# Gate rows of a three-layer kernel: by way of DRAM in place of VectorE and PE

## The reference

```python
def adaln(cond, w, b):
    return jnp.split(jax.nn.silu(cond) @ w + b, 6, axis=-1)

def modulate(x, shift, scale):
    return rms_norm(x) * (1.0 + scale) + shift
```

## Time and profile before

| | before |
|---|---|
| median of three runs | 3646.86 us |
| profiled execution | 3648.11 us |
| span of its instructions | 3646.3 us |
| PE busy | 3121.2 us (86%) |
| VectorE busy | 1479.6 us (41%) |
| ScalarE busy | 889.9 us (24%) |
| GpSimd busy | 290.6 us (8%) |
| DMA queue of SP | 190288 packets, 647.72 MB |
| granted TensorE clock, mean | 0.92 |
| `gate_rows` on VectorE, L552 (64 instructions) | 12.9 us |

### The profile page before, as it was taken

One profiled execution on the slowest core, in us unless ns is written; L12 is line 12 of the kernel. 1 busy time (PEld: TensorE's weight loads), 2 busy tenths in 40 slices (PEclk: granted clock), 3 DMA queues, 4 the chain that ended last, 5 costly groups with the idle time before them and its releaser, 6 DMA issues. The chain is left out here.

```text
span 3646.3 us, 95140 instructions
## 1 busy us (share of the span) xinstructions
PE 3121.2 (86%) x42406; PEld 2257.6 (62%) x42406; DVE 1479.6 (41%) x2409; ACT 889.9 (24%) x1501; POOL 290.6 (8%) x241
## 2 busy tenths in 40 slices
PE   6978879997877888787897956676999999999996
PEld 3855558886565666674786945533566666666663
DVE  3355653333663554546565885524111111111111
ACT  2114322222222343331343532301000011100000
POOL 0020200000311132230000013100000000000000
PEclk7989789999898999997998967887999999999998
DMA  7252332222133100103653520221999999999993
GB/s 285 82 172 81 133 139 93 93 93 93 45 142 124 50 21 29 42 4 124 231 185 119 196 82 3 100 98 38 399 408 407 405 405 406 406 406 408 406 405 148
DMA packets 220725, 684.12 MB, mean 188 GB/s; under 512 B 26096, under 2 KB 51184, under 8 KB 187712
## 3 DMA queue, kind: packets, MB, share of 16 engines
q1 hardware_dynamic: 190288, 647.72, 46.4%
q10 hardware_dynamic: 30192, 32.77, 2.6%
HBM read 659.46 MB, written 20.97 MB: 187 GB/s over the span
## 5 line engine op out<-in xcount | busy, mean ns | idle before, releaser
L3466 PE MATMUL experts_psum_gu<-ring,experts_x 128*32 128x256 f32 x9216 | 507.6, 381 | 13.8 <-ACT experts_x L3510 13.8
L3466 PEld LDWEIGHTS experts_psum_gu<-ring,experts_x 128*32 128x32 f32 x9216 | 296.8, 111 | 216.2 <-ACT experts_x L3510 15.4
L3570 DVE TENSOR_TENSOR experts_gate<-experts_psum_gu,experts_bias 128x768 f32<-128x768 f32 x32 | 30.6, 957 | 863.9 <-PE experts_psum_gu L3466 863.9
L3489 PE MATMUL experts_psum_down<-experts_weights,experts_hiddenT 128*32 128x256 f32 x6144 | 339.1, 381 | 4.2 <-ACT experts_hiddenT L3518 4.2
L3489 PEld LDWEIGHTS experts_psum_down<-experts_weights,experts_hiddenT 128*32 128x32 f32 x6144 | 200.6, 111 | 136.8 <-issue 6.0
L818 PE MATMUL mlp_psum_bank<-mlp_x_high,mlp_w_high 128*128 128x512 f32 (+1 forms) x512 | 175.6, 343 | 12.6 <-DVE xT_rounded L322 12.6
L296 DVE TENSOR_TENSOR ring_rounded<-ring,mlp_w_high 128x1024 fp32r<-128x1024 f32 x128 | 156.7, 1226 | 50.6 <-ACT mlp_w_high L291 50.5
L3514 ACT ACTIVATE experts_sigmoid<-experts_gate 128x768 f32<-128x768 f32 x32 | 27.0, 843 | 615.3 <-DVE experts_gate L3572 615.3
L818 PE MATMUL mlp_psum_bank<-xT_rounded,mlp_w_high 128*128 128x512 f32 (+1 forms) x512 | 173.8, 339 | 0.0
L818 PE MATMUL mlp_psum_bank<-mlp_x_high,ring_rounded 128*128 128x512 f32 (+1 forms) x512 | 173.2, 338 | 0.0
L3466 PE MATMUL experts_psum_gu<-xT,experts_x 128*32 128x256 f32 x3072 | 171.6, 379 | 0.0
(11 more groups left out here) (724 smaller groups left out, 5796.5 us busy)
## 6 DMA issues: line engine op xcount, KB each, us to landing
ring<-in_w_gu SPq DMA_DIRECT2D x186, 1024.0 KB, 18.0
experts_weights<-in_w_down SPq DMA_DIRECT2D x128, 1024.0 KB, 19.4
ring<-in_ada_w SPq DMA_DIRECT2D x36, 2048.0 KB, 8.7
ring<-in_mlp_w SPq DMA_DIRECT2D x32, 2048.0 KB, 8.0
xT<-in_w_gu SPq DMA_DIRECT2D x64, 1024.0 KB, 18.9
ring<-in_w_in SPq DMA_DIRECT2D x12, 2048.0 KB, 7.6
ring<-in_ab_w_in SPq DMA_DIRECT2D x6, 2048.0 KB, 9.7
ring<-in_w_rkv SPq DMA_DIRECT2D x6, 2048.0 KB, 8.5
```

Source lines behind the costliest of these rows:

```text
L3466: mm = nc.tensor.matmul(pg[o, q, gr, :], x, w[:, c:c + C], start=(u == 0 and gr != 1), stop=(u == U - 1), skip_group_check=True)
L3489: mm = nc.tensor.matmul(pd[o, gr, :], hidT[:, ch, gr, GROUP * v:GROUP * v + GROUP], w[:, ch, C * c:C * c + C], start=(v == 0 and ch == 0 a ...
L3570: v.tensor_tensor(gt[:, :, :], pg[:, 0, 0:GROUPS, :], rep(bias[:, 0, :], GROUPS), ALU.add).then_inc(s_bg, 1)
```

## The change

The four `gate_rows` phases are gone. In their place each gate takes two DMA steps on SP's queue. First its columns are stored to a row of DRAM (`gate_out`): the source is 128 x 8 single values, one every 8 bytes in a partition, the target has the values of one partition 512 bytes apart, so that the store is made of 1024 pieces of 4 bytes. Later, in another phase, the row of 4 KB is read to all 128 partitions (`gate_in`, 512 KB for a gate). Where `rows1` stood, a `load` phase is left that does the same loads as before.

| gate | stored in | loaded in |
|---|---|---|
| layer 0, four | `mlrows`, after `sel` and `head_row`, ahead of the bias and the ring loads | `about`, ahead of the ring loads |
| layer 1, two | `norm1a` | `rwout`, ahead of the ring loads |
| block 2, mixer | `norm2a`, last of the Fetch | `gdmerge`, with `sn` |
| block 2, experts | `mixout`, ahead of the ring loads | `norm2m`, last of the Fetch |

`gemm_tok` gets a Fetch: SP issues it first, and VectorE waits for it ahead of the first output tile. In `gemm_rows` and in `norm1a` SP waits for the store at the end of its program.

```diff
@@ class Fetch
-        for dst, src in self.jobs:
-            eng.dma_start(dst, src).then_inc(self.sem, 16)
+        for dst, src, *by_element in self.jobs:
+            eng.dma_start(dst, src, allow_slow_non_contiguous=bool(by_element)).then_inc(self.sem, 16)
@@ gemm_tok(..., fetch=None)
             def _(sync):
+                if fetch is not None:
+                    fetch.issue(sync)
                 ring.issue(sync, len(chunks))
...
                         dve.wait_ge(ring.gemm_done, done0 + n + 1)
+                        if n == 0 and fetch is not None:
+                            fetch.wait(dve)
                         out(ch, t, c0, w, banks[:, n % 8, 0:w]).then_inc(evac, 1)
@@
-def gate_rows(g, name, cols, rows, fetch=None):
...
+def gate_out(g, dram, layer, gates):
+    return [(dram[n].rearrange("(k p) -> p k", p=P).unsqueeze(2), g.mods[layer % 2][:, 8 * j:8 * j + 8, i:i + 1], True) for n, j, i in gates]
+
+def gate_in(dram, rows, gates):
+    return [(rows[:, k, :], row(dram[n])) for k, n in enumerate(gates)]
@@ gemm_rows(..., fetch)
             def _(sync):
+                fetch.issue(sync)
                 ring.issue(sync, n_chunks)
+                fetch.wait(sync)
@@ layer0
-                       Fetch(g, "ldsel", [(sel[:, :, :], a["sel"]), (head_row[:, :], row(a["headn"]))]),
+                       Fetch(g, "ldsel", [(sel[:, :, :], a["sel"]), (head_row[:, :], row(a["headn"]))]
+                             + gate_out(g, gate_d, 0, ((0, 2, 0), (1, 2, 1), (2, 5, 0), (3, 5, 1)))),
...
-        gate_rows(g, "rows0", [lambda kt, j=j, i=i: g.mods[0][:, 8 * j + kt, i:i + 1] for j, i in
-                               ((2, 0), (2, 1), (5, 0), (5, 1))], rows)
         gemm_tok(g, "about", widths(D), (g.xT, g.xT_low), ALL_TILES,
-                 residual(g, lambda t: rows[:, 0 if t >= 2 else 1, :], 0))
+                 residual(g, lambda t: rows[:, 0 if t >= 2 else 1, :], 0), fetch=Fetch(g, "ldgate0", gate_in(gate_d, rows, range(4))))
@@ layer1
+    norm_T(g, "norm1a", ALL_TILES, g.xT, lambda t: mod(1, t), lambda t: mod(0, t),
+           fetch=Fetch(g, "stgate1", gate_out(g, gate_d, 1, ((0, 2, 0), (1, 5, 0)))))
...
-            gate_rows(g, "rows1", [lambda kt, j=j: g.mods[1][:, 8 * j + kt, 0:1] for j in (2, 5)], rows,
-                      Fetch(g, "ldro", [(g2a[:, :], a["g2"][0:P, :]), (g2b[:, :], a["g2"][P:G_LORA, :])]
+            load(g, "ldro", [(g2a[:, :], a["g2"][0:P, :]), (g2b[:, :], a["g2"][P:G_LORA, :])]
...
-                     residual(g, lambda t: rows[:, 0, :], 0))
+                     residual(g, lambda t: rows[:, 0, :], 0), fetch=Fetch(g, "ldgate1", gate_in(gate_d, rows, range(2))))
@@ block2
                                              (small[:, :], row(a["small2"])), (gn[:, :], row(a["gdn_norm_g"]))]
+                               + gate_out(g, gate_d, 2, ((0, 2, 0),))))
...
+                gd_merge(..., Fetch(g, "ldmix", [(sn[:, :], row(a["ssd_norm_g"]))] + gate_in(gate_d, rows, (0,))),
...
-                gate_rows(g, "rows2", [lambda kt: g.mods[0][:, 16 + kt, 0:1]], rows)
-                gemm_rows(g, "mixout", 4, mixT, rows[:, 0, :])
+                gemm_rows(g, "mixout", 4, mixT, rows[:, 0, :], Fetch(g, "stgate3", gate_out(g, gate_d, 2, ((1, 5, 0),))))
...
+                   fetch=Fetch(g, "ldmoe", [(rb[:, :], row(a["router_b"])), (iota[:, :], row(a["iota"]))] + gate_in(gate_d, rows, (1,))))
-            gate_rows(g, "rows3", [lambda kt: g.mods[0][:, 40 + kt, 0:1]], rows)
```

More of the change, by code:

```diff
@@ L326, in get, with gemm_tok @@
         return self.hi[:, kt, sl], self.x_low[:, kt, sl]
-def gemm_tok(g, name, chunks, acts, tiles, out, depth=8):
+def gemm_tok(g, name, chunks, acts, tiles, out, depth=8, fetch=None):
     nc, ring = g.nc, g.ring
@@ L3117, in _, with gemm_rows @@
                 m.add(dve)
-def gemm_rows(g, name, n_chunks, actT, row):
+def gemm_rows(g, name, n_chunks, actT, row, fetch):
     nc, ring = g.nc, g.ring
@@ L3694, in layer0 @@
     nc = g.nc
+    gate_d = nc.dram_tensor("gates_0", [4, D], F32, kind="Internal").ap()
     first_modulation(g, "ada0", (a["cond_col"], a["cond2_col"]), a["adab_col"][0], ident, const, x_in)
@@ L3756, in layer1 @@
     mod = lambda j, t: g.mods[1][:, 8 * j:8 * j + 8, 0 if t >= 2 else 1]
-    norm_T(g, "norm1a", ALL_TILES, g.xT, lambda t: mod(1, t), lambda t: mod(0, t))
     scr = {n: nc.dram_tensor(f"rw_{n}", [2 if n == "r" else 4, P, D], F32, kind="Internal").ap()
            for n in ("k", "v", "kk", "r")}
+    gate_d = nc.dram_tensor("gates_1", [2, D], F32, kind="Internal").ap()
+    norm_T(g, "norm1a", ALL_TILES, g.xT, lambda t: mod(1, t), lambda t: mod(0, t),
+           fetch=Fetch(g, "stgate1", gate_out(g, gate_d, 1, ((0, 2, 0), (1, 5, 0)))))
     with ExitStack() as outer:
@@ L3801, in layer1 @@
             roT_low = rounded_alias(nc, roT)
-            gate_rows(g, "rows1", [lambda kt, j=j: g.mods[1][:, 8 * j + kt, 0:1] for j in (2, 5)], rows,
-                      Fetch(g, "ldro", [(g2a[:, :], a["g2"][0:P, :]), (g2b[:, :], a["g2"][P:G_LORA, :])]
-                            + [(v[:, t, :], scr["v"][2 + t]) for t in range(2)]
-                            + [(lw[:, :], row(a["lnx_w"])), (lb[:, :], row(a["lnx_b"]))]))
+            load(g, "ldro", [(g2a[:, :], a["g2"][0:P, :]), (g2b[:, :], a["g2"][P:G_LORA, :])]
+                 + [(v[:, t, :], scr["v"][2 + t]) for t in range(2)]
+                 + [(lw[:, :], row(a["lnx_w"])), (lb[:, :], row(a["lnx_b"]))])
             rw_readout(g, y, coef, v, {"lw": lw[:, :], "lb": lb[:, :]}, sg0, sg1, g2a, g2b, ro,
@@ L3817, in block2 @@
     nc = g.nc
+    gate_d = nc.dram_tensor("gates_2", [2, D], F32, kind="Internal").ap()
     mod = lambda j, t: g.mods[0][:, 8 * j:8 * j + 8, 0]
@@ L3829, in block2 @@
                    fetch=Fetch(g, "ldconv", [(gains[:, :, :], a["norm_g_col"]), (taps[:, :, :], a["taps_col"]), (cbias[:, :], a["cbias_col"]),
-                                             (small[:, :], row(a["small2"])), (gn[:, :], row(a["gdn_norm_g"]))]))
+                                             (small[:, :], row(a["small2"])), (gn[:, :], row(a["gdn_norm_g"]))]
+                               + gate_out(g, gate_d, 2, ((0, 2, 0),))))
             p2 = msb("proj2", [P, 2, 2080])
@@ L3862, in block2 @@
                 sn = isb("sn", [P, D])
-                gd_merge(g, p2, og, ys, {"gn": gn[:, :], "sn": sn[:, :]}, mix, Fetch(g, "ldmix", [(sn[:, :], row(a["ssd_norm_g"]))]),
+                rows = isb("gate_rows2", [P, 1, D])
+                gd_merge(g, p2, og, ys, {"gn": gn[:, :], "sn": sn[:, :]}, mix, Fetch(g, "ldmix", [(sn[:, :], row(a["ssd_norm_g"]))] + gate_in(gate_d, rows, (0,))),
                          (2, 8, 4, a["adab2_col"]))
@@ L3867, in block2 @@
                                   for t in range(2) for k in range(16)])
-                rows = isb("gate_rows2", [P, 1, D])
-                gate_rows(g, "rows2", [lambda kt: g.mods[0][:, 16 + kt, 0:1]], rows)
-                gemm_rows(g, "mixout", 4, mixT, rows[:, 0, :])
+                gemm_rows(g, "mixout", 4, mixT, rows[:, 0, :], Fetch(g, "stgate3", gate_out(g, gate_d, 2, ((1, 5, 0),))))
         acc = osb("moe_acc", [P, 2, D])
@@ L3881, in block2 @@
             norm_T(g, "norm2m", LAT_TILES, g.xT, lambda t: mod(4, t), lambda t: mod(3, t), gains[:, 1, :], off=2,
-                   fetch=Fetch(g, "ldmoe", [(rb[:, :], row(a["router_b"])), (iota[:, :], row(a["iota"]))]))
-            gate_rows(g, "rows3", [lambda kt: g.mods[0][:, 40 + kt, 0:1]], rows)
+                   fetch=Fetch(g, "ldmoe", [(rb[:, :], row(a["router_b"])), (iota[:, :], row(a["iota"]))] + gate_in(gate_d, rows, (1,))))
             router(g, a["router_w"], rb[:, :], iota[:, :], a["b_down"], acc, rank[:, :, :], topg[:, :, :], XgT,
```

## The result

The changed kernel is slower, by little. Its median is 3650.07 us (20 runs, 3643.34 to 3658.74) against 3642.46 us for the kernel before (20 runs, 3635.29 to 3650.76): ratio 1.002, 95% interval 1.0012 to 1.0028, thus 7.3 us slower, from 4.4 to 10.2. The profiled execution took 3649.26 us.

The account below looks back on a forecast made before the run. Phases end in barriers, so wall time between barriers, not PE's 86% busy time, was taken to price the change. 21.4 - 1.6 - 5.2 - 2.0 = 12.6 us less, from 3646.9 to 3634.3 us; range 3627 to 3652.

Parts of the forecast that it names:

- The phases that go: Wall time saved by removing the four `gate_rows` phases: 12.0 + 0 + 3.7 + 5.7 = 21.4 us.
- clock charge: At the start of `mixout`, PE would run some 3.3 us at half clock after the pause, costing 1.7 us.
- The loads of the rows: Rows loaded in `about`, `rwout` and `gdmerge` would be hidden, 0 each; the one in `norm2m` would cost 1.6 us.
- S: Time one store of 1024 4-byte pieces takes on the queues: taken as 2.0 us, bounds 1.0 to 5.5.
- -(4S - 2.8): In `mlrows`, four stores ahead of the ring load delay the fourth slice: -5.2 us, bounds -1.2 and -19.2.
- low bound: Time per store from below, by comparing the loads `router_w` and `gains`: 1024 pieces take about 1.0 us more than none.
- The room of 2.8 us: In `mlrows`, free queue time between `head_row` leaving the engines at about 349.0 and the ring load beginning at 351.8.
- The signs named beforehand: Prediction wrong if a lone store takes 6 us or more, SP is held issuing one, or VectorE waits in `about`.
- "Slower": Rival: writes of neighbouring values wait for each other, felt in `mlrows`' queue; S = 7 gives 3659.3 us; chance 0.10.
- "Even": Rival: S is 3.1 to 6.0, both DMA waits give back the savings; S = 4.5 gives 3646.9 us; chance 0.18.

Follow-up runs that it names:

- e2: The kernel before with only the four layer 0 stores added to `mlrows`, read by nothing; 3665.79 us against 3650.02, ratio 1.0047.
- e4: The kernel before with four loads by element (1024 pieces of 4 bytes each) added in `mlrows`, no stores; 3652.36 us, ratio 1.0008.
- e6: The kernel before with four stores added in `mlrows`, their values 64 bytes apart in DRAM instead of 4; 3649.68 us, ratio 1.0007.
- e9: The kernel before with two of the four stores added in `mlrows`; single execution, PE's wait there 9.2 us, whole time not read.
- e10: The kernel before with four stores of eight 512-byte pieces each added in `mlrows`; single execution, SP held 1.33 us, whole time not read.
- e8: The changed kernel, unchanged, profiled a second time; waits 16.9 us in `mlrows` and 8.4 us in `norm2a`, whole time not read.
- e12: The changed kernel, unchanged, profiled a third time; `mlrows` to `mlstm` took 38.4 us, whole time not read.
- e3: The changed kernel with layer 0's stores moved to `mlstm` and `norm2a`'s store in a Fetch of its own; 3637.31 us, ratio 0.9965.
- e5: The changed kernel with layer 0's stores in `mlstm` and `norm2a`'s store at the start of `mlp1`; 3627.45 us against 3645.08, ratio 0.9954.

## Why the prediction was wrong, point by point

- **The phases that go.** `rows0` 12.0 us: right. From the first turn of `turnD` to `about` it was 17.3 us before and 5.3 after, in the means of three; the 11.5 of the table, which starts at `abmerge`, is less because `abmerge` itself varies. `rows1` 0: measured 0, the loads did set its end. `rows3` with the added row of 512 KB, 5.7 - 1.6 = 4.1: measured 5.5 and 5.1, because VectorE's wait grew from 2.90 to only 3.18; the second row's transfer ran beside the first's. `rows2`: 5.4 less a clock charge of 1.7 gave 3.7, measured 5.2 and 4.7. The charge was wrong: `mixout` took 61.5 us up to `norm2m`, against 61.8 before, so it lost nothing at its start. PE had the full clock there (the sixth value behind the length of the stretch), though it had idled for 1.68 us just before:

```profile
2386.00:2387.00 1.00, 0.54 (x2) 0.33 (x3) 0.00 (x0) 0.00 (x0) 0.00 (x0) 1.00 0.00 0
2387.00:2388.00 1.00, 1.00 (x4) 0.52 (x3) 0.00 (x0) 0.00 (x0) 0.00 (x0) 1.00 0.48 4
```

- **The loads of the rows.** `about`, `rwout` and `gdmerge` made nothing wait, as said: in `about` VectorE's first output came 15.2 us after the phase's start against 14.6, and was released by PE.
- **The step that failed: S = 2.0**, the time of one store on the queue, and with it the wait -(4S - 2.8) in `mlrows`. The prediction took twice the low bound, "nearest to `router_w`" in number and smallness. Put back into its formula, the waits give 4.2 (e2), and 4.3 from the changed kernel's own wait (16.92 - 2.41 = 4S - 2.8). `mlrows` lost 14.5 us and not 5.2. But the mechanism was wrong too, not only the size: the pieces of a store are through the engines in about 1 us, as the low bound had it. The loss was a ring load slowed behind them (7.6 us) and issued later (6.9 us). The row chosen was a load; e4 shows that such loads would have cost 1.6 us in all. What the prediction named as its doubt, neighbouring values that come from different partitions, is what e6 points to: spread, the same stores cost 2.9 us. The room of 2.8 us was perhaps read a little wide as well: the slices of the earlier trace rows show some traffic until 349.75, which would leave 2.1.
- **`norm2a`: not S at all.** It was priced as the time that one store takes on the queues, 2.0 us, and lost 6.9. A wait for a store ends with its landing, 8.6 us for a lone one, while its packets are through in 1. Time on the queue and time to landing are two quantities; the model had one.
- **SP.** Four issues were priced at 0.4 us each, and fit ahead of the ring's. One store, and in e9 two, did take 0.4 to 0.5 us each; four held SP for 6.62 us and the bias behind them for 4.20, and moved the ring load's issue.
- **The signs named beforehand.** A lone store at 6 us or more, and SP held up: both came (8.6 us; 6.62 us). The third, VectorE waiting for the rows in `about`, did not. Packets under 512 B rose by 8448, which is the 8192 pieces and 16 more for each of the 16 new DMAs.
- **The rivals.** "Slower" had the mechanism that e6 bears out, writes of neighbouring values that hold each other up, but its price, S = 7, was too high. "Even" had the price, S from 3.1 to 6.0: 22.6 - 5 x 4.3 = 1.1 us less. What the touched stretches show in the mean is 1.5 us more. That the kernel is slower and not even rests on stretches in which it removed nothing. In the three profiles these are 2.0 us in `about` and `norm0m`, and +4.6 in the RWKV chunks against -3.8 elsewhere, which may be chance; why the twenty runs are 7.3 apart and the profiles 4.3 stays open.
- **The range** held 3650.07; the direction and the chance of 0.10 for slower were wrong. That it held was luck in part: it was built on 3646.86, the median of three runs, and the twenty have 3642.46. Moved down by these 4.4 us it would have ended at 3647.6. A forecast with S at the middle of its bounds (3.3) would have been 6 us less, within what the prediction counted as even.

The rule of the Trainium skill that was quoted against the change (page "DMA: Bandwidth & Descriptors", specifications: a transfer below 512 bytes is a read-modify-write) fits that writes were dear and loads cheap. It does not tell neighbours from spread values; e2 and e6, equal in the size of their pieces, differ by 11 us of wait, and the measurement decides.

## What to carry to other kernels

A store made of 4-byte pieces that lie side by side in DRAM is slow to land, and cheap to issue only while few stand in a row: place it in a phase where no load that anyone waits for is near it on the queue, before or behind. Long pieces were free here (e10); what it would cost to turn the data first was not measured. Spreading the targets 64 bytes apart took away most of the cost (e6), though the rows would then have to be read from spread values, which was not tried. When an operation is absent from a trace, take the nearest row in the direction of the transfer too, and price separately how long it holds the queue, how long it holds the issuing engine, and how long until it lands. And a phase removed is worth its wall time only if what it did does not come back in front of a load that already ends a wait.

## What the runs showed of the hardware

- A store of 1024 pieces of 4 bytes, 4 bytes apart in DRAM: through the DMA engines in about 1 us, landed after 8.6 us (alone; 8.2 and 8.3 in e8 and e12). Four such stores slow a following load to 30 to 70 GB/s for some 7 us; 64 bytes apart they cost 2.9 us of wait instead of 14.1.
- A load of 64 KB issued 0.47 us before such a store landed after 9.7 us instead of 2.9 (e3), and after 7.0 in the changed kernel; in the same phase without a store it took 2.9 again (e5).
- Four DMAs of 1024 pieces hold SP for about 4.5 us whether they load or store spread values (e4: 4.55, e6: 4.50), and for 5.2 to 6.6 in `mlrows` when they store neighbours; two such stores for 1.05 (e9), four of eight pieces for 1.33 (e10).
- A second broadcast row of 512 KB behind a first added 0.3 us to the wait for both.
